# Mixer of a two-layer block: eleven long taps in the input projection, latent roots on four columns, mixed rows copied by ScalarE, first exponentials ahead of value copies

## The reference, cut to what matters

```python
h = rmsnorm(x, mix_norm[i]) @ w_in[i]
y_mla  = mla_mixer(...)             # 8 heads of softmax attention, on latents that are rms-normed first
y_conv = conformer_conv_mixer(...)  # a * sigmoid(g), depthwise conv of 31 taps, layernorm, silu
y_hy   = hyena_mixer(...)           # depthwise conv of 3 taps, then twice: long conv by FFT, gate
y = concatenate([rmsnorm(y_mla, ..), rmsnorm(y_conv, ..), rmsnorm(y_hy, ..)])
x = x + y @ w_out[i]
# in mla_mixer:
q = (rmsnorm(h_q, q_norm) @ w_qb)     # h_q: 256 channels
kv = (rmsnorm(h_kv, kv_norm) @ w_kvb) # h_kv: 128 channels
```

## Time and profile before

| | us |
|---|---|
| median of three runs | 3454.01 (3450.14 to 3454.5) |
| the profiled execution's own time | 3450.73 |
| its span, first to last instruction | 3448.9 |
| TensorE busy | 3290.9 (95%) |
| VectorE busy | 1798.8 (52%) |
| ScalarE busy | 751.6 (22%) |
| GpSimd busy | 1829.8 (53%) |
| chain that ended last: TensorE / VectorE / issue / ScalarE | 82% / 12% / 3% / 2% |

### The profile page before, as it was taken

The page is one execution under the profiler, slowest core; times in us unless marked ns, Lnnn a source line. Parts: engine busy times, 40 slices in busy tenths (PEclk is TensorE's granted clock), DMA queues, the critical chain, the costliest instruction groups (busy, mean ns, idle before and its releaser), DMA issues.

```text
span 3448.9 us, 43775 instructions
## 1 busy us (share of the span) xinstructions
PE 3290.9 (95%) x14400; PEld 2568.7 (74%) x14400; DVE 1798.8 (52%) x1995; ACT 751.6 (22%) x1265; POOL 1829.8 (53%) x1026
## 2 busy tenths in 40 slices
PE   6999999989999999999989999999998999999997
PEld 5788875468887788876457888777777777788886
DVE  6642168663312753138855331576767886753313
ACT  2110025522211111013432220111122322222201
POOL 4556651056666646653026666544454455666664
PEclk9999999999999999999999999999999999999998
DMA  4222330023333322331012332322222222223332
GB/s 138 80 79 93 97 104 19 7 80 96 95 95 99 108 74 86 97 110 55 13 37 92 96 94 96 112 74 65 65 83 67 69 67 73 90 93 94 95 97 73
DMA packets 77141, 280.98 MB, mean 81 GB/s; under 512 B 9350, under 2 KB 9734, under 8 KB 76360
## 3 DMA queue, kind: packets, MB, share of 16 engines
q1 hardware_dynamic: 74016, 268.84, 24.5%
q10 hardware_dynamic: 2984, 10.27, 0.9%
HBM read 276.97 MB, written 2.10 MB: 81 GB/s over the span
## 4 chain that ended last, share of the span: by engine, by line
PE 82%; DVE 12%; issue 3%; ACT 2%; DVEq 0%; ACTq 0%; DMA 0%; SPq 0%
PE bank L497 24%; PE bank L502 24%; PE bank L501 24%; DVE xbc L2137 1%; DVE x_lo L1620 1%; PE bank L714 1%; PE bank L778 1%; PE bank L632 1%; PE bank L796 1%; PE bank L702 1%; DVE scaled L1972 1%; DVE square_sum L1630 1%; DVE ssm_lo L1774 1%; PE bank L609 0%; DVE y L1860 0%
## 5 line engine op out<-in xcount | busy, mean ns | idle before, releaser
L443 POOL TENSOR_SCALAR w_hi<-raw 128x1024 fp32r<-128x1024 f32 x504 | 550.9, 1093 | 1539.8 <-PE bank L497 1532.5
L446 POOL TENSOR_TENSOR w_lo<-raw,w_hi 128x1024 fp32r<-128x1024 f32 x504 | 1266.4, 2513 | 42.0
L497 PE MATMUL bank<-x_hi,w_hi 128*128 128x512 f32 x2896 | 1151.9, 398 | 69.9 <-DVE x_lo L1620 31.1
L502 PE MATMUL bank<-x_hi,w_lo 128*128 128x512 f32 x2896 | 1134.2, 392 | 0.0
L501 PE MATMUL bank<-x_lo,w_hi 128*128 128x512 f32 x2896 | 1134.0, 392 | 0.0
L497 PEld LDWEIGHTS bank<-x_hi,w_hi 128*128 128x128 f32 x2896 | 548.0, 189 | 210.0 <-issue 77.9
L501 PEld LDWEIGHTS bank<-x_lo,w_hi 128*128 128x128 f32 x2896 | 548.1, 189 | 117.0 <-issue 5.1
L502 PEld LDWEIGHTS bank<-x_hi,w_lo 128*128 128x128 f32 x2896 | 547.4, 189 | 116.2
L502 PE MATMUL bank<-hidden_hi,w_lo 128*128 (+1 forms) x880 | 347.6, 395 | 0.0
L497 PE MATMUL bank<-hidden_hi,w_hi 128*128 (+1 forms) x880 | 347.6, 395 | 0.0
L501 PE MATMUL bank<-hidden_lo,w_hi 128*128 (+1 forms) x880 | 347.6, 395 | 0.0
(11 more groups left out here) (369 smaller groups left out, 3244.8 us busy)
## 6 DMA issues: line engine op xcount, KB each, us to landing
raw<-in_w SPq DMA_DIRECT2D x504, 512.0 KB, 3.5
dft<-in_dft ACTq DMA_DIRECT2D x2, 1536.0 KB, 6.9
x<-in_x SPq DMA_DIRECT2D x2, 1024.0 KB, 7.0
out<-x SPq DMA_DIRECT2D x4, 512.0 KB, 2.6
mask<-in_mask ACTq DMA_DIRECT2D x1, 1536.0 KB, 7.4
filt_cos<-in_dft_filter ACTq DMA_DIRECT2D x2, 512.0 KB, 5.5
filt_sin<-in_dft_filter ACTq DMA_DIRECT2D x2, 512.0 KB, 7.3
sel<-in_sel ACTq DMA_DIRECT2D x1, 768.0 KB, 4.9
```

The source lines that it names most:

```text
L443: nc.gpsimd.tensor_scalar(w_hi[:, s % 2, :], raw[:, s, :], 1.0, 0.0, ALU.mult, ALU.add).then_inc(w_rounded, 1)
L446: nc.gpsimd.tensor_tensor(w_lo[:, s % 2, :], raw[:, s, :], w_hi[:, s % 2, :].bitcast(F32), ALU.subtract).then_inc(w_split, 1)
L497: first = nc.tensor.matmul(out, hi_w, hi, start=start, stop=False)
L502: return nc.tensor.matmul(out, lo_w, hi, start=False, stop=stop)
```

## The change

- **Taps.** The 31-tap conv's instructions for its first half, taps 0 to 10, move from the heads into the input projection: two while the squares of the query latents are made, four after `norm_summed`, two after the reciprocal, three ahead of the second gate product. The second pair of tiles is taken out later by that. 51 taps stay, a half in turn; slots of the heads are filled from the first on, so the last eleven are empty.
- **Latent roots.** A sum of squares is made with the squares as weights and one column of ones as input, four matmuls, giving 128 x 4 numbers. ScalarE's root and VectorE's reciprocal work on these. Inside tiles 5 and 7, after two of eight pieces, TensorE spreads them again over 128 rows with four matmuls against `ident`, and VectorE multiplies the latents with that bank.
- **Mixed rows.** The copies of heads 0 to 6 go from VectorE to ScalarE, placed behind the scalings of the next head. Head 7's stays.
- **Exponentials.** The first two of head 0 go ahead of the two copies of values, and a one-column exponential (`exp_warm`) stands ahead of `mla_inputs(0)`.
- **Spectrum products.** Two pairs of products of 256 columns become one of 512 each, four times a layer.

```diff
-            def in_projection(tiles, between):
+            def in_projection(tiles, inside, between):
                 for n in range(tiles):
                     pe.wait_ge(tile_free, c.next(tile_free))
+                    to = bank[RING[n % len(RING)]][:]
+                    if n in inside:
+                        s = take()
+                        project_part(to, s, 0, 2)
+                        inside[n]()
+                        project_part(to, s, 2, DC).then_inc(tile_ready, 1)
...
+                def latent_sums(n):
                     if n == 2:
-                        after(norm_rms, 1)
+                        after(latent_scaled, 1)
                     after(norm_summed, n)
-                    nc.tensor.matmul(bank[SUM_BANK][:], ones[:], (square_sum[:] if n > 1 else square[:, 0, :]),
-                                     start=True, stop=True).then_inc(norm_sum, 1)
+                    for t in range(TT):
+                        last = nc.tensor.matmul(bank[SUM_BANK][:, t:t + 1],
+                                                (square_sum if n > 1 else square[:, 0])[:, t * P:(t + 1) * P],
+                                                ones[:, 0:1], start=True, stop=True)
+                    last.then_inc(norm_sum, 1)
+
+                def latent_spreads(n):
+                    after(latent_inverted, n)
+                    for t in range(TT):
+                        last = nc.tensor.matmul(bank[SUM_BANK][:, t * P:(t + 1) * P],
+                                                latent_root[:, t:t + 1].broadcast_to([P, P]), ident[:],
+                                                start=True, stop=True)
+                    last.then_inc(latent_spread, 1)
+
+                in_projection(IN_BLOCKS, {5: lambda: latent_spreads(1), 7: lambda: latent_spreads(2)},
+                              {1: sum_squares, 4: lambda: latent_sums(1), 6: lambda: latent_sums(2)})
+                after(latent_scaled, 2)
...
# ScalarE
+                def latent_norm(srcs, width):
...
+                    nc.scalar.activation(latent_root[:], bank[SUM_BANK][:, 0:TT], ACT.Sqrt, bias=eps[:],
+                                         scale=1.0 / width).then_inc(norm_rms, 1)
...
                     for t in range(2):
+                        if g == 0:
+                            exponential(0, t)
                         act.wait_ge(v_ready, c.next(v_ready))
...
+                def mixed(h):
+                    act.wait_ge(mixed_ready, c.next(mixed_ready))
+                    nc.scalar.activation(y[(h % 2) * V_DIM:(h % 2 + 1) * V_DIM, 4 + h // 2, :],
+                                         bank[MIX_BANK][0:V_DIM, :], ACT.Copy).then_inc(mixed_copied, 1)
...
                 odd_half(0, 0)
+                nc.scalar.activation(exp_warm[:], eps[:], ACT.Exp)
                 mla_inputs(0)
-                for t in range(TT):
+                for t in range(2, TT):
                     exponential(0, t)
...
                 mla_square(0)
                 over_sums(3)
+                mixed(2)
                 head(3, second_signal)
...
                 over_sums(7)
+                mixed(6)
+                c.add(mixed_ready)
                 act.wait_ge(norm_in, c.next(norm_in))
...
# VectorE
+                def latent_inverse():
+                    dve.wait_ge(norm_rms, c.next(norm_rms))
+                    nc.vector.reciprocal(latent_root[:], latent_root[:]).then_inc(latent_inverted, c.add(latent_inverted))
+
                 def latent_scale(tiles, at):
-                    dve.wait_ge(norm_rms, c.next(norm_rms))
-                    link(nc.vector.reciprocal(mix_rms[:], mix_rms[:]))
+                    dve.wait_ge(latent_spread, c.next(latent_spread))
...
+                early = 11
+                tap_order = [(0, j) for j in range(early)]
+                for j in range(TAPS):
+                    tap_order.append((1, j))
+                    if early + j < TAPS:
+                        tap_order.append((0, early + j))
...
+                latent_inverse()
+                gate_tiles()
+                latent_scale((2,), KV_NORM)
+                gate_product(0)
+                norm_squares(2, lambda: long_taps(2))
+                long_taps(4)
+                latent_inverse()
+                long_taps(2)
+                latent_scale((0, 1), Q_NORM)
+                dve.sem_inc(latent_ready, 1)
+                gate_tiles()
+                long_taps(3)
+                gate_product(1)
+                short_tile(0)
...
-                    nc.vector.tensor_tensor(first[0], re, f_re, ALU.mult)
-                    nc.vector.tensor_tensor(first[1], im, f_im, ALU.mult)
+                    nc.vector.tensor_tensor(products[:, 0:2, :].rearrange("p a n -> p (a n)"), low,
+                                            spectrum[:, k, o, :], ALU.mult)
...
# in head(h) of VectorE
                     invert_sums(h + 1)
                     last_unit()
-                    mixed(h)
```

More of the change, by code:

```diff
@@ L246, in build @@
         row_inv = sb("row_inv", [P, TT], F32, mix_mem)
+        latent_root = sb("latent_root", [P, TT], F32, mix_mem)
+        exp_warm = sb("exp_warm", [P, 1], F32, mix_mem)
         conv_mem = ExitStack()
@@ L398, in build @@
         rope_ready = sem("rope_ready")
+        latent_inverted, latent_spread, latent_scaled = (
+            sem(n) for n in ("latent_inverted", "latent_spread", "latent_scaled"))
         q_ready, q_copied, k_ready, k_copied, v_ready, v_copied, q_roped = (
@@ L1815, in short_tile, with long_tap, long_taps, tap @@
                                                             short[:, i, :], ALU.mult, ALU.add))
+                def latent_inverse():
+                    dve.wait_ge(norm_rms, c.next(norm_rms))
+                    nc.vector.reciprocal(latent_root[:], latent_root[:]).then_inc(latent_inverted, c.add(latent_inverted))
                 def latent_scale(tiles, at):
-                    dve.wait_ge(norm_rms, c.next(norm_rms))
-                    link(nc.vector.reciprocal(mix_rms[:], mix_rms[:]))
+                    dve.wait_ge(latent_spread, c.next(latent_spread))
                     for n, i in enumerate(tiles):
-                        link(nc.vector.scalar_tensor_tensor(latent[:, i, :], latent[:, i, :], col(at + n),
-                                                            mix_rms[:], ALU.mult, ALU.mult))
+                        last = nc.vector.scalar_tensor_tensor(latent[:, i, :], latent[:, i, :], col(at + n),
+                                                              bank[SUM_BANK][:], ALU.mult, ALU.mult)
+                    link(last, latent_scaled)
+                early = 11
[4 more added lines that the diff above has]
+                        tap_order.append((0, early + j))
+                taken, tap_at = [0], [None, None]
+                def long_tap():
+                    i, j = tap_order[taken[0]]
+                    taken[0] += 1
+                    if j:
+                        dve.wait_ge(dve_step, tap_at[i])
+                    acc, w, src = conv_acc[:, i, :], col(CONV_W + i * TAPS + j), long_pad[:, i, j:j + T]
+                    if j == 0:
+                        ins = nc.vector.tensor_scalar(acc, src, w, col(CONV_B + i), ALU.mult, ALU.add)
+                    else:
+                        ins = nc.vector.scalar_tensor_tensor(acc, src, w, acc, ALU.mult, ALU.add)
+                    ins.then_inc(dve_step, c.add(dve_step))
+                    tap_at[i] = c.at(dve_step)
+                def long_taps(n):
+                    for _ in range(n):
+                        long_tap()
+                def tap():
+                    if taken[0] < 2 * TAPS:
+                        long_tap()
                 for i in (2, 0, 1):
@@ L2012, in mixer @@
                 head(5, lambda: spectrum_terms(1, 1), lambda: spectrum_sums(1, 1))
-                while taken[0] < 2 * TAPS:
-                    long_tap()
+                long_taps(2 * TAPS - taken[0])
                 dve.wait_ge(dve_step, tap_at[1])
```

67 lines of the change are left out of this document (28 added, 39 removed).

## The result

The changed kernel takes 3463.85 us (median of 7 runs, 3463.2 to 3467.16) against 3454.01 (7 runs): 1.0033 times the kernel before, 95% interval 1.0022 to 1.0043. It is 9.84 us slower: 0.85 us above the upper end of my range (3445 to 3463), on the side to which I had given 0.2. The profiled execution has a span of 3462.1 us at a mean clock of 0.986; before it was 3448.9 at 0.989. The two profiled spans differ by 13.2 us, more than the medians.

What follows compares the result with a forecast made beforehand. TensorE paces the projection; no engine binds throughout the heads. Terms sum to -0.75 us in layer 1 and +0.9 in layer 2, +0.15 on 3450.73; with 3.28 to the median, 3454.2 us. Range 3445 to 3463.

Steps and rivals of the forecast that it cites:

- the projection: Input projection: latent roots 2.2 us a layer slower (1.92 of TensorE work, 0.3 of wait); the eleven taps hidden.
- head 2's copy: Behind head 2: ScalarE's copy, queued after head 3's scalings, delays TensorE and mla_inputs(1); 1.1 us a layer slower.
- the heads 3 to 7: Predicted for heads 3 to 5: fewer taps and copies on VectorE, 2.85 us a layer faster, limited by TensorE's idle running.
- the exponentials: Head 0: earlier first exponentials shorten waits of TensorE and VectorE; 2.25 us gained in layer 1, 0.6 in layer 2.
- the spectrum products: Heads 0 and 1: two products of 256 columns become one; 0.1 us a layer faster, between 0 and 0.3.
- head 6's copy: Behind head 6: ScalarE's copy delays the squares and the chain to the output projection; 1.15 us a layer slower.
- the wait ahead of the second spread: Projection, tile 7: TensorE waits 0.3 us for the latent root's reciprocal, behind four taps on VectorE.
- the rival: Projection: fourth tap stands for a GpSimd split ahead of the reciprocal; 3.9 us a layer slower, 3462; chance 0.18.
- the second rival: Projection and heads: waits shrink and the clock falls with them, including head 3 of layer 2; 3447; chance 0.19.
- The gain of 0.7: End of head 3: VectorE's copy is gone, 0.7 us saved.
- The vanished wait of 1.84: Head 5: TensorE's 1.84 us wait before the inverse transform goes; the idle running is then late next.
- The 0.86 in head 4: Head 4: the last product's 0.86 us wait is gained, as it then waits only for the idle running.

## Why the prediction was wrong

My sum for the two layers was +0.15, the traces have +13.3. The 13.15 between them are 4.05 in the projection, 3.66 at head 2's copy, 5.54 in the heads 3 to 7, 0.38 at the exponentials, less 0.45 at the spectrum products and 0.03 at head 6's copy. So three steps of the sum failed: the price of the longer wait for head 2's copy, the wait ahead of the second spread, and the clock in head 3, which I had put at nothing. The order of events was as walked in most places; what it costs when the clock falls was left out of the sum.

- **Head 2's copy (3.66 of 13.15).** The order on ScalarE and the added wait were as walked, 1.3 in place of 1.1. The term was mis-sized because I left the clock in a side clause, "1.7 more should the longer wait at head 3 end in the lower clock", outside the sum. A wait of 2.64 us there had it fall in all twelve layers that show one (step +2.0 to +3.3), against -0.2 in the ten where the copy went ahead and 1.3 in the two that were filled. 1.1 should have been 2.9.
- **The taps before the second reciprocal (4.05).** I took 0.3 us of wait as likely and gave the tap that stands for a split 0.18. The walk was right to within 0.1 us in layer 1. But I measured the margin at the wrong place: the fourth tap against the subtraction, half a microsecond, and not the third against the rounding, where it was 0.2 us or less. 7 layers of 10 fell on the far side, 3.7 to 4.8 us each (4.1 in the mean) more than the three others, as the rival had priced it (3.9). By this share, counted afterwards and in ten layers only, 0.7 x 4.1 = 2.9 us a layer belonged in the sum, 5.7 in all.
- **Head 3's clock (most of 5.54).** Not in my sum, only half in the second rival, where I had the fall disappear. It fell in both layers of the changed kernel and in one of before, in the profile. The gain of 0.7 that I had for the copy at its end is there, as 0.5 (17.39 against 17.90 us without a fall, 18.08 against 18.57 with the filled wait), and went under in the fall: -0.5 + 3.0 = +2.5 in layer 1; in layer 2, where before had one of 1.6, +0.9. Measured: +2.49 and +0.85. That before's layer 1 had none looks like luck of its profile, since 18 of the 20 layers with this wait have one. Why the fall cost more in the changed kernel stays open.
- **Exponentials.** Right in size, -2.08 / -0.39, and partly by luck: 1.7 of layer 1 is a clock fall that the old order has in half of its layers (3 of 6). Against a median of before I estimate 0.4 + 0.85 a layer at this step; of the 0.4 next to nothing is left at head 5, and no time shows it.
- **Heads 4 and 5.** The vanished wait of 1.84 is there (-1.88), and that idle running is late next is shown by the kernel with less of it (2.4 us more). The 0.86 in head 4 is not: that wait is still 0.50 us, and the next maximum came 0.14 later.
- **Head 6's copy.** +1.13 / +1.14 against 1.15; back on VectorE 0. The wait of 1.90 us that it makes brought the clock down in 4 of the 16 layers that have it, and the step was +1.71 to +2.21 there: a price that my sum doesn't have and that the changed kernel's profile doesn't show.
- **Spectrum products, table load.** -0.3 instead of -0.1 (no run has this edit alone); the load of 1.28 us was hidden as said.
- **Sum against the median.** I added 3.28 us to pass from the profiled execution to the median. For a kernel whose clock falls by chance this is a term of its own: before's profiled execution was one of the luckier ones (12 of its 86 runs, which range over 3445 to 3464 us, are as fast or faster), after's is at its median. So profiles differ by 13.2 and medians by 9.84.

In the traces the later of the two was the one that was stretched, whichever engine it was. The tap behind the rounding took 1.54 us and the one behind the subtraction 2.61, in place of 0.75. Where the tap was first, the rounding took 1.46 in place of 1.04. The subtraction of layer 2 took 2.66 in place of 2.39, and the third tap was still running (to 1556.08) when it began at 1555.63. The Trainium skill ("SBUF — State Buffer", Who interferes with whom) says that whichever of VectorE and GpSimd issues first keeps the shared port and the other blocks. The trace agrees on who waits; where GpSimd was the later one it was stretched by 0.4 and 0.3 us, with 0.56 and 0.45 us of the tap left to run.

What stays open is why the clock falls behind one wait and not behind its like. In the 22 layers with small roots it fell right behind the wait of 1.62 to 1.67 us ahead of the second sums in 19, and in the other three behind the next wait, of 3.37, 0.86 and 0.44 us. The records show that it fell, not why.

## What to carry to other kernels

Price an edit that lengthens a TensorE wait with the clock that may fall behind it, by the rows of like waits in all layers, not of one. A fall seen once in two layers is a chance, to be entered with its share on both sides. Where your walk puts an instruction half a microsecond from the edge beyond which it stands for another engine's, take the edge as passed as often as not, and keep short work that others wait for ahead of it. Measure the margin at every instruction of the other engine's chain, not only at the longest. When VectorE gets free, look for idle running that was sized to the old lateness. It must shrink with it, or it takes the gain.

## What the runs showed of the hardware

- The same wait in the same place mostly had both outcomes. Behind 2.10 us the clock fell in 3 layers of 6, behind 2.86 us in 18 of 20, behind 1.90 us at the tail in 4 of 16; behind 2.64 us at head 2's copy in 12 of 12. Where the wait of 2.64 or 2.86 us was filled with unread matmuls (2 and 8 layers), the clock didn't fall behind it.
- VectorE's reciprocal of 128 x 4 took 0.16 to 0.18 us against 3.35 of 128 x 512; four one-column sums 0.95 to 1.28 us at TensorE in the changed kernel, where I had 0.92, and four spreads 1.05 to 1.13 where I had 1.06. In other profiles, at the lower clock, the spreads took up to 2.05.
- ScalarE's copy of a 64 x 512 bank tile takes 0.57 to 0.59 us, VectorE's 0.68: the engine hardly matters, the queue ahead of it does.
